# Seven block products in place of eight in 14 input slabs of a feed-forward, with the weight sums made by GpSimd

## The reference, cut to what matters

```
def swiglu(h, w_in, w_out):
    g, u = jnp.split(h @ w_in, 2, axis=-1)
    return (jax.nn.silu(g) * u) @ w_out

def ffn_sublayer(x, g, shift, scale, gate, w_in, w_out):
    return x + FFN_RES * gate * swiglu(modulate(rms_norm(x, g), shift, scale), w_in, w_out)
```

## Time and profile before

| | us |
|---|---|
| median of 3 runs (1643.31 to 1643.63) | 1643.58 |
| span of the profiled execution | 1641.7 |
| PE busy in it | 1619.9 |
| DVE busy | 1117.3 |
| ACT busy | 603.0 |
| POOL busy | 119.3 |

### The profile page before, as it was taken

How to read it: one execution, slowest core, us unless ns; L and a number is a source line. 1 busy time by engine, 2 the same in 40 slices (tenths; PEclk the granted TensorE clock), 3 DMA queues, 4 the chain that set the end, 5 groups by cost and what they waited for, 6 DMA issues and landing times.

```text
span 1641.7 us, 23536 instructions
## 1 busy us (share of the span) xinstructions
PE 1619.9 (99%) x8838; PEld 1389.5 (85%) x8838; DVE 1117.3 (68%) x1837; ACT 603.0 (37%) x824; POOL 119.3 (7%) x80
## 2 busy tenths in 40 slices
PE   9999999999998999999999999999999999999998
PEld 6788888889877898888888898888888898999997
DVE  5878777778489588777777773563333687676665
ACT  3321222234688433212212342222222356544443
POOL 0000000000698000000000000000000012000000
PEclk8999999999999999999999999999999999999999
DMA  8755555543211236555555322432222232155552
GB/s 329 276 199 178 199 202 193 187 164 111 78 52 52 78 118 242 180 191 204 192 192 181 139 96 89 174 128 102 103 77 102 103 106 77 59 188 202 185 198 78
DMA packets 45283, 246.41 MB, mean 150 GB/s; under 512 B 5152, under 2 KB 5280, under 8 KB 24992
## 3 DMA queue, kind: packets, MB, share of 16 engines
q1 hardware_dynamic: 45216, 245.50, 41.6%
...
## 4 chain that ended last, share of the span: by engine, by line
PE 88%; DVE 4%; POOL 3%; ACT 2%; issue 2%; DMA 1%; SPq 0%; DVEq 0%; ACTq 0%; POOLq 0%
PE ps L1862 13%; PE ps L1864 13%; PE ps L1871 13%; PE ps L1692 10%; PE ps L1694 10%; PE ps L1693 10%; PE ps L2369 5%; PE ps L1719 4%; PE ps L2375 2%; POOL spare L587 2%; PE ps L1988 1%; PE ps L1900 1%; DVE w_lo L1251 1%; PE ps L2284 1%; PE ps L2041 1%
## 5 line engine op out<-in xcount | busy, mean ns | idle before, releaser
L1862 PE MATMUL ps<-a_hi,w_hi 128*128 128x512 f32 x960 | 373.8, 389 | 0.8 <-ACT w_hi L716 0.8
L1864 PE MATMUL ps<-a_lo,w_hi 128*128 128x512 f32 x960 | 373.5, 389 | 0.0
L1251 DVE TENSOR_TENSOR w_lo<-raw,w_hi 128x2048 fp32r<-128x2048 f32 x112 | 256.1, 2287 | 49.1 <-ACT w_hi L716 21.7
L1692 PE MATMUL ps<-h_hi,w_lo 128*128 128x512 f32 (+1 forms) x648 | 235.0, 363 | 0.1
L1693 PE MATMUL ps<-h_lo,w_hi 128*128 128x512 f32 (+1 forms) x648 | 233.4, 360 | 0.0
L1694 PE MATMUL ps<-h_hi,w_hi 128*128 128x512 f32 (+1 forms) x648 | 233.4, 360 | 0.0
L1871 PE MATMUL ps<-a_hi,w_lo 128*128 128x512 f32 x960 | 227.3, 389 | 0.0
L1862 PEld LDWEIGHTS ps<-a_hi,w_hi 128*128 128x128 f32 x960 | 180.2, 188 | 38.9 <-issue 0.8
L1864 PEld LDWEIGHTS ps<-a_lo,w_hi 128*128 128x128 f32 x960 | 180.2, 188 | 37.4
L1871 PEld LDWEIGHTS ps<-a_hi,w_lo 128*128 128x128 f32 x960 | 180.2, 188 | 37.4
L710 ACT ACTIVATE work<-ps 128x512 f32<-128x512 f32 x66 | 39.5, 598 | 432.3 <-PE ps L1871 419.3
...
## 6 DMA issues: line engine op xcount, KB each, us to landing
raw<-wstream SPq DMA_DIRECT2D x146, 1024.0 KB, 4.9
mring<-wmod SPq DMA_DIRECT2D x144, 512.0 KB, 3.5
spare<-wstream SPq DMA_DIRECT2D x11, 1024.0 KB, 4.8
...
cb<-cond SPq DMA_DIRECT2D x1, 1024.0 KB, 7.8
...
```

The lines of the kernel that those rows point to most:

```text
L1251: dve.tensor_tensor(w_lo[:, slot], raw[:, slot], w_hi[:, slot].bitcast(F32), ALU.subtract).then_inc(lo_ready, 1)
L1692: pe.matmul(dst, lhs_lo, rhs_hi, start=start, stop=False, skip_group_check=True)
L1862: pe.matmul(bank, hi, a_hi[:, k, 0:nt], start=k == 0, stop=False, skip_group_check=True)
L1864: pe.matmul(bank, hi, a_lo[:, k, 0:nt], start=False, stop=False, skip_group_check=True)
```

## The change

In groups 1 and 2 of `ffn2` (`FAST`; 8 and 6 slabs) the product of an input slab is done by blocks. Split the inner dimension in two halves of 4 feature tiles, the output in gate and up, and the 512 tokens in two halves `b`, each with 128 latent and 128 context tokens. A 2 x 2 by 2 x 2 block product then needs seven block products instead of eight, if sums of the weight blocks and sums of the token blocks are formed first and the results are combined afterwards (Strassen, in Winograd's form). A block product is 4 feature tiles times 3 passes: 12 matmuls of 128 x 256, seven times, 84 in all, in the order P0 to P6 of `fast_slab`.

- **Token sums**, once: `token_sums` and `token_lows` (VectorE) and four copies on ScalarE make `t_hi`, `t_lo` during the output slabs after group 0.
- **Weight sums**, per slab: the four adds of 128 x 512 in `weight_sums` on GpSimd, written in place into `raw` and the new `extra`.
- **Splits**, per slab: seven quarters stand for four. They are made in four parts (512, 1024, 1024 and 1024 columns) by `part_high` on ScalarE and `part_low` on VectorE, into a ring of seven quarters that lies over both slots of `w_hi` and `w_lo`, so there is one slab's worth of room, and a part is overwritten as soon as its products are done.
- **Combination**, per slab: a PSUM copy on ScalarE (`gate_copy1`) and five VectorE instructions of 128 x 256 (`neg_u2`, `neg_u3`, two for `up_sum`, `gate2`). SiLU is done in two halves, and `prod` is now a product of two SBUF tensors, since the up part lies in `up_sum`.
- **Transfers**: each of the 14 slabs comes in two transfers, one quarter into `extra` and three into `raw`.
- **Moved**: the last modulation dots of `ffn2`'s first output slabs go to the first four input slabs of its group 0.

The last slab of each fast group (`ahead` false) prepares an ordinary output slab instead of parts.

```diff
@@ -65,7 +65,22 @@
 MOD_STEPS = FFN_SLABS - 4
-MOD_PHASES = ((0, 1, 2, 3, 4), (0, 1, 2, 3, 4), (1,), ())
+MOD_PHASES = ((0, 1, 2, 3, 4), (0, 1, 2, 3, 4), (), ())
...
+QUARTER = SLAB // 4
+RING = (slice(0, QUARTER), slice(QUARTER, 3 * QUARTER), slice(3 * QUARTER, 5 * QUARTER),
+        slice(5 * QUARTER, 7 * QUARTER))
+N_COMB, N_PROD = 5, 6
+T_ORDER, T_PLACE = (0, 2, 1, 3), (0, 1, 3, 2)
...
+        def part_source(part, p):
+            return (extra[:, p, 2 * QUARTER:3 * QUARTER], extra[:, p, 0:2 * QUARTER], raw[:, p, 0:2 * QUARTER],
+                    raw[:, p, 2 * QUARTER:SLAB])[part]
...
+            def quarter_loads(w, p, wait):
+                sp.wait_ge(lo_ready, wait)
+                sp.dma_start(extra[:, p, 2 * QUARTER:3 * QUARTER],
+                             wstream[ds(w, 1), :, 3 * QUARTER:SLAB].rearrange("a p n -> p (a n)")) \
+                  .then_inc(fast_loaded[p], 16)
+                sp.dma_start(raw[:, p, 0:3 * QUARTER],
+                             wstream[ds(w, 1), :, 0:3 * QUARTER].rearrange("a p n -> p (a n)")) \
+                  .then_inc(raw_loaded[p], 16)
...
+            def weight_sums(n, w):
+                p = n % 2
+                pool.wait_ge(fast_loaded[p], 16 * (n // 2 + 1))
+                pool.wait_ge(raw_loaded[p], 16 * (w // 2 + 1))
+                a22, a21, a12, s4 = (raw[:, p, c * QUARTER:(c + 1) * QUARTER] for c in range(4))
+                s2, s3, a11 = (extra[:, p, c * QUARTER:(c + 1) * QUARTER] for c in range(3))
+                pool.tensor_tensor(s3, a11, a21, ALU.add).then_inc(col_added, 1)
+                pool.tensor_tensor(a21, a21, a22, ALU.add).then_inc(row_added, 1)
+                pool.wait_ge(col_added, n + 1)
+                pool.tensor_tensor(s2, s3, a22, ALU.add).then_inc(three_added, 1)
+                pool.wait_ge(three_added, n + 1)
+                pool.tensor_tensor(s4, s2, a12, ALU.add).then_inc(four_added, 1)
...
+            def part_high(part, n, w, p, i=None):
+                if part == 0:
+                    act.wait_ge(fast_loaded[p], value_at(i, 8, 16 * (n // 2 + 1)))
+                if part == 1:
+                    act.wait_ge(three_added, value_at(i, 1, n + 1))
+                if part == 2:
+                    act.wait_ge(row_added, value_at(i, 1, n + 1))
+                if part == 3:
+                    act.wait_ge(four_added, value_at(i, 1, n + 1))
+                act.activation(ring_hi[:, RING[part]], part_source(part, p), ACT.Copy) \
+                   .then_inc(hi_ready if part == 3 else part_hi, 1)
+            def fast_step(w, f, n, q, i=None, ahead=True):
+                p = n % 2
+                act.wait_ge(prod_done, value_at(i, N_PROD, N_PROD * n + 1))
+                act.activation(gate_copy1, ps[GATE1_BANK[p]][:, 0:LAT], ACT.Copy).then_inc(first_copied, 1)
+                if ahead:
+                    part_high(0, n + 1, w + 1, 1 - p, i)
+                    act.wait_ge(prod_done, value_at(i, N_PROD, N_PROD * n + 3))
+                    part_high(1, n + 1, w + 1, 1 - p, i)
+                    act.wait_ge(prod_done, value_at(i, N_PROD, N_PROD * n + 5))
+                    part_high(2, n + 1, w + 1, 1 - p, i)
+                else:
+                    act.wait_ge(prod_done, N_PROD * n + 4)
+                    split_hi(w + 1, (w + 1) % 2, w + 1)
+                act.wait_ge(prod_done, value_at(i, N_PROD, N_PROD * n + 6))
+                act.activation(sil[:, p, 0:LAT], ps[GATE1_BANK[p]][:, 0:LAT], ACT.Silu)
+                act.wait_ge(slab_done, value_at(i, 1, w + 1))
+                if ahead:
+                    part_high(3, n + 1, w + 1, 1 - p, i)
+                else:
+                    split_hi(w + 2, w % 2, w + 2)
+                act.wait_ge(combined, value_at(i, N_COMB, N_COMB * n + 5))
+                act.activation(sil[:, p, LAT:TOK], gate2, ACT.Silu).then_inc(sil_ready, 1)
+                act.wait_ge(pair_free, value_at(i, 1, f + 3))
+                dst = h_hi[:, q] if i is None else h_hi[:, ds(i + q, 1)].rearrange("p a n -> p (a n)")
+                act.activation(dst, prod[:, p], ACT.Copy).then_inc(hhi_ready, 1)
...
+            def part_low(part, n, w, p, i=None):
+                if part == 3:
+                    dve.wait_ge(hi_ready, value_at(i, 1, w + 1))
+                else:
+                    dve.wait_ge(part_hi, value_at(i, 3, 3 * n + part + 1))
+                dve.tensor_tensor(ring_lo[:, RING[part]], part_source(part, p), ring_hi[:, RING[part]].bitcast(F32),
+                                  ALU.subtract).then_inc(lo_ready if part == 3 else part_lo, 1)
...
+            def fast_step(w, f, n, q, i=None, ahead=True, behind=True):
+                p = n % 2
+                def product(k):
+                    dve.wait_ge(prod_done, value_at(i, N_PROD, N_PROD * n + k))
+                def earlier(k):
+                    dve.wait_ge(combined, value_at(i, N_COMB, N_COMB * n + k))
+                if ahead:
+                    part_low(0, n + 1, w + 1, 1 - p, i)
+                product(2)
+                dve.wait_ge(first_copied, value_at(i, 1, n + 1))
+                dve.tensor_tensor(neg_u2, ps[ODD_BANK][:, 0:LAT], gate_copy1, ALU.subtract).then_inc(combined, 1)
+                if behind:
+                    hidden_low(f - 1, 1 - p, q - 1, i)
+                product(3)
+                earlier(1)
+                dve.tensor_tensor(neg_u3, neg_u2, ps[MID_BANK][:, 0:LAT], ALU.subtract).then_inc(combined, 1)
+                if ahead:
+                    part_low(1, n + 1, w + 1, 1 - p, i)
+                product(4)
+                earlier(2)
+                dve.tensor_tensor(up_sum[:, 0:LAT], neg_u3, ps[ODD_BANK][:, 0:LAT], ALU.subtract).then_inc(combined, 1)
+                product(5)
+                dve.tensor_tensor(up_sum[:, LAT:TOK], neg_u3, ps[GATE2_BANK][:, 0:LAT],
+                                  ALU.subtract).then_inc(combined, 1)
+                if ahead:
+                    part_low(2, n + 1, w + 1, 1 - p, i)
+                else:
+                    split_lo(w + 1, (w + 1) % 2)
+                dve.wait_ge(slab_done, value_at(i, 1, w + 1))
+                dve.tensor_tensor(gate2, ps[GATE2_BANK][:, 0:LAT], neg_u2, ALU.subtract).then_inc(combined, 1)
+                if ahead:
+                    part_low(3, n + 1, w + 1, 1 - p, i)
+                dve.wait_ge(sil_ready, value_at(i, 1, f + 1))
+                earlier(4)
+                dve.tensor_tensor(prod[:, p].rearrange("p (v b n) -> p b v n", v=2, b=2),
+                                  sil[:, p].rearrange("p (b v n) -> p b v n", v=2, b=2),
+                                  up_sum.rearrange("p (b v n) -> p b v n", v=2, b=2), ALU.mult).then_inc(pair_free, 1)
...
+            def token_sums(j):
+                p0, p1, p2, p3 = (part_view(x) for x in t_parts)
+                if j == 0:
+                    for dst, kk, b in ((p0, 0, 0), (p1, 0, 1), (p3, 1, 1)):
+                        last = dve.tensor_tensor(dst, tile_part(a_hi[:].bitcast(F32), kk, b),
+                                                 tile_part(a_lo[:].bitcast(F32), kk, b), ALU.add)
+                    link(last)
+                    dve.tensor_tensor(p0, p0, p1, ALU.subtract).then_inc(t_sum, 1)
+                else:
+                    dve.tensor_tensor(p1, p3, p1, ALU.subtract).then_inc(t_sum, 1)
+                    link(dve.tensor_tensor(p2, tile_part(a_hi[:].bitcast(F32), 1, 0),
+                                           tile_part(a_lo[:].bitcast(F32), 1, 0), ALU.add))
+                    dve.tensor_tensor(p3, p3, p0, ALU.add).then_inc(t_sum, 1)
+                    dve.wait_ge(t_sum, 3)
+                    dve.tensor_tensor(p2, p3, p2, ALU.subtract).then_inc(t_sum, 1)
...
+            def fast_slab(w, f, n, i):
+                p = n % 2
+                gate1, gate2_bank, odd, mid = (ps[c][:, 0:LAT] for c in (GATE1_BANK[p], GATE2_BANK, ODD_BANK, MID_BANK))
+                def plain_part(kk, b):
+                    return lambda x, k: token_part(x[0][:, 4 * kk + k], b)
+                def sum_part(c):
+                    return lambda x, k: x[1][:, c, k]
+                def comb(k):
+                    pe.wait_ge(combined, i * N_COMB + (N_COMB * n + k))
+                def product(r, bank, moving, start, end):
+                    ready = (0, 1, 1, 2, 2, 3, 3)[r]
+                    for high in (True, False):
+                        if r in (0, 1, 3, 5):
+                            if ready == 3:
+                                pe.wait_ge(hi_ready if high else lo_ready, i + (w + 1))
+                            else:
+                                pe.wait_ge(part_hi if high else part_lo, i * 3 + (3 * n + ready + 1))
+                        for k in range(4):
+                            c0 = r * QUARTER + k * P
+                            for x in ((a_hi, t_hi), (a_lo, t_lo)) if high else ((a_hi, t_hi),):
```

(28 more changed lines are left out.)

260 lines of the change are left out of this document (199 added, 61 removed).

## The result

| | before | after |
|---|---|---|
| device time, median (range) | 1643.61 us (1643.31 to 1643.90, 4 runs) | 1665.74 us (1665.27 to 1668.19, 4 runs) |
| ratio after/before, 95% interval | | 1.0135, 1.0121 to 1.0150 |
| span of the profiled execution | 1641.7 us | 1663.2 us |

The change makes the kernel 22 us slower, within 0.3 us of the forecast.

What follows compares the result with a forecast made beforehand. PE bounds the kernel, busy 1619.9 of 1641.7 us. 1643.6 - 11.2 (shorter slabs) + 17.7 (waits ahead of P3) + 0.5 (group ends) + 15.5 (GpSimd's adds) gave 1666.1 us, own range 1659 to 1674.

Steps and rivals of the forecast that it cites:

- PE's steps: Matmuls of 256 columns step at 0.120 us in all seven products, saving 0.80 us a slab, 11.2 in all.
- The chain to P3: ScalarE and VectorE work up to neg_u2 makes PE wait 1.59 us ahead of P3 in middle slabs, 17.7 in all.
- The register waits: Waits against registers between the steps ahead of P3: 0.1 to 0.2 us more a slab possible, left to the range.
- Holding off: A GpSimd add and a VectorE instruction with two SBUF operands hold each other off for a whole instruction: 15.5 us.
- side by side: Rival: GpSimd's adds and VectorE's instructions do not hold each other off; 1650.6 us, or 1652.5 with register waits; chance 0.26.
- Its price: One GpSimd add met in each slab that prepares a next one: 12 x 1.29 = 15.5 us.
- two adds in the chain: Rival: low part 3 and prod are each held by an add, 7.0 + 31.0, about 1681 us; chance 0.09.
- The faster rival: The work up to P3 takes less than 5.12 us, so slabs save up to 11.2 us (1632.4); chance 0.08.
- At nothing: Token sums and moved dots on VectorE, and the second transfer per slab, were priced at no cost.
- After it nothing is late.: Behind P3 in each slab, P4, P5 and P6 find their inputs ready, so PE waits nowhere else.

Runs made afterwards that it cites:

- kernel 8: The kernel after with neg_u2 ahead of low part 0 (VectorE), gate_copy1 ahead of h_hi (ScalarE), and GpSimd's adds replaced by memsets: 1632.8 us.
- kernel 1: The kernel after with GpSimd's four weight-sum adds per slab replaced by memsets, which read nothing: 1652.1 us.
- kernel 2: The kernel before with four GpSimd adds put beside each of the 14 input slabs, results unchanged: 1643.6 us.
- kernel 6: The kernel after, order unchanged, with up_sum and prod in PSUM banks in place of SBUF: 1655.1 us.
- kernel 7: The kernel after with neg_u2 ahead of low part 0, gate_copy1 ahead of h_hi, and up_sum and prod in PSUM: 1637.35 us.
- kernel 9: As kernel 7, but VectorE does low part 1 of the next slab behind both halves of up_sum: 1637.0 us.

## Why the prediction was right, and where it was not

- **PE's steps.** Right. 0.120 in every product; kernel 8 is at 1632.8 against 1632.9 by the steps alone.
- **The chain to P3.** Right to 0.05 us a slab: 1.64 against 1.59 in kernel 1, and all waits of the kernel after stand ahead of P3, released by `neg_u2`. 18.3 us against 17.7. The register waits, allowed 0.1 to 0.2, can be at most that 0.05. Kernel 1 is 8.5 us slower than before where 18.3 + 0.5 - 11.2 gives 7.6. The other 0.9 lies ahead of these slabs: its profiled execution comes to group 1 at 1084.14, where before came at 1082.79 and kernel 8, with the same program up to there, at 1082.58. From there to the end of group 2 kernel 1 takes 203.6 us against 195.8, 7.8 more.
- **Holding off.** The mechanism is right and was the uncertain part (0.26 stood for side by side). Kernels 1, 2 and 6 show it three ways.
- **Its price was mis-sized.** "I take one add met in each slab that prepares a next one: 12 x 1.29 = 15.5 us." Measured, the waits grew by 9 us. In the ten middle slabs the idle time above the 1.39 of kernel 1 is 1.69, 0, 1.08, 0.74, 1.36, 0 in group 1 and 1.69, 0, 1.08, 0.74 in group 2: 8.4 us, so seven slabs of ten are hit and three not at all (another 0.65 is in the first slab of group 1). In these seven, ten instructions are held, low part 3 five times and `prod` five times. So the count, one a slab, came out right on average, and each cost 0.84: an instruction that comes up while an add runs waits for its rest, not for 1.29 (0.3 to 0.7 in low part 3, 1.1 in `prod`), and an add that arrives second is itself held and costs VectorE nothing by that.
- **A term was missing.** The clock: waits near 3 us bring PE to the lower level for 16 matmuls, 4.4 us. The prediction never asked what PE's own speed would be after a wait. No slab of before makes PE wait for long, but its trace has the thing once, in the mixer of layer 0 (timeline of PE, then a stretch of 4 us as above), and none of the prediction's rows shows it:

```profile
514.79 1.51 PE L2140 MATMUL ps<-ab_pt,ab_v 128*64 128x128 f32 x16 [2.17 <-ACT rspread L886]
515.00:519.00 4.00, 4.00 (x29) 3.43 (x26) 3.63 (x12) 3.45 (x10) 3.69 (x4) 0.57 0.76 262
```

After 2.17 us of waiting the granted clock is 0.57. So a row of before could have warned; "two adds in the chain" was priced with such waits at full clock. The two errors, 6.4 too much and 4.4 too little, mostly cancel. The 2.0 that are left are made up by 0.6 more in the chain and by the 1.0 by which the medians lie farther apart (22.1) than the parts add up (21.1). That the total is right to 0.3 us is luck.
- **The faster rival** (chance 0.08) named its own condition, a chain below 5.12, and its price, 1632.4. Kernel 8 meets the first and comes within 0.4 of the second.
- **At nothing.** The moved dots, token sums and the second transfer cost nothing that shows: the only wait of PE outside P3 in this stretch is 0.2 at a group's exit, and the transfers land after 5.0 and 3.6 us, as the earlier trace rows would have it:

```profile
raw<-wstream SPq DMA_DIRECT2D x14, 768.0 KB, 5.0
extra<-wstream SPq DMA_DIRECT2D x14, 256.0 KB, 3.6
```

- **"After it nothing is late."** True for this kernel, and no longer once the chain is mended: in kernel 7 it is P6 that comes 0.26 late, in kernel 9 P3 again.
